# Expert stage of a two-block model: GpSimd asks for U and V rows one by one in turn, where a group asked for two of U and then two of V

## The chip, the cores and the metric

One Trainium2 chip, one of its cores. The time of a kernel is the device time of that core in microseconds (us), taken as the median of several runs. A profile is one further execution, recorded by the hardware profiler.

## The reference, cut to what matters

The model has two blocks of two layers each. The change touches the feed-forward of the first block, a mixture of 16384 experts per layer with 128 chosen for each token:

```python
def block(args):                       # 128 tokens
    hk, ek, gk = args                  # hk [128, 1024], ek, gk [128, 128]
    act = jax.nn.gelu(jnp.einsum('ted,td->te', u[ek], hk), approximate=False)
    return jnp.einsum('te,ted->td', gk * act, v[ek])
```

For each token and each of its 128 experts, one row of U (1024 floats, 4 KB) is multiplied with the token's row, and one row of V is added to the output with a weight. The experts come from eight heads with two top-16 searches and a top-16 of their sums each. Layer 0 does this for 512 tokens (256 of the context and 256 of x), layer 1 for 256 tokens: six tiles of 128 tokens.

## The kernel before, in words

The 128 tokens of a tile lie on the 128 partitions. A request is one indirect DMA that GpSimd issues. It brings the n-th expert's row for each of the 128 tokens: 128 rows of 4 KB, 524288 bytes, into one buffer. There are 6 buffers for U and 6 for V (`U_SLOTS`, `V_SLOTS`; only 4 for U while a projection still runs beside the first groups). Six tiles with 128 experts make 768 requests for U and 768 for V.

The work goes in groups of two experts (`GROUP = 2`), 384 groups in all. Each engine runs its own program in its written order and waits on semaphores:

- **GpSimd (POOL)** in group g waits until the dots of group g-3 have freed two U buffers (`dots_done`) and asks for two U rows (L1746). Then it waits until the weighing three groups before has freed two V buffers (`v_weighed`) and asks for the two V rows of group g-2 (L1756; `LAG = 2`).
- **VectorE (DVE)** waits for each U row in turn and multiplies and sums it with the token rows (L1782, called a dot here, one for each expert); after the second it signals `dots_done`. Then it multiplies the previous group's gelu by the gates (L1791), and does a piece of the searches for the experts of later groups (`keys.chunk`), in 13 of every 16 groups.
- **ScalarE (ACT)** in group g takes the gelu of the two dots (L1833), and then makes two diagonal matrices for group g-2 (L1842). So the diagonals of group g-2 come only after the dots of group g.
- **TensorE (PE)** weighs: it multiplies each diagonal by its V row into PSUM (L1890), four products of 128x512 a group, eight rows in the trace, and signals `v_weighed`.

SP loads the weights of the other stages, 2 MB apiece, through its own queue. In the first part of layer 0's expert stage it also loads the modulation weights (`w_mod`), which TensorE uses beside the experts.

The first groups of each layer run beside the projection and ask for U alone; the groups that follow catch up with three groups of V at a time. After that each turn of the loop asks for one group of U and one of V. The change is in these turns.

Of the kernel before, what the change touches and what calls it, by code (L numbers as in the profile page):

```python
# [330 lines left out]
class Angles:  # L331
# [51 lines left out]
    def gpsimd(self, pool):  # L383
        A = self.A
        pool.wait_ge(self.m.sines.sem, 1)
        for k in range(2):
            pool.tensor_scalar(A.sin[:, k, :], self.ang[:, 2 * k, :], A.const[:, C_SIGN + k:C_SIGN + k + 1], None, ALU.mult)
            pool.tensor_copy(A.cos[:, k, :], self.ang[:, 2 * k + 1, :])
# [1270 lines left out]
GROUP = 2  # L1659
U_FIRST = 4  # L1660
U_SLOTS = 6
V_SLOTS = 6
# [5 lines left out]
class Experts:  # L1668
# [63 lines left out]
    def turned(half):  # L1732
        return half // 4, slice((half % 4) * P, (half % 4 + 1) * P)

    def ask_u(self, pool, g):
        m = self.m
        if g % self.some == 0:
            pool.wait_ge(m.keys_done.sem, self.keys.base[m.keys_done] + g // self.some + 1)
            pool.sem_inc(m.rows_asked.sem, 1)
        needed = max(self.u_dots_needed(g * GROUP + r) for r in range(GROUP))  # L1740
        if needed:
            pool.wait_ge(m.dots_done.sem, self.at(m.dots_done, needed))
            pool.sem_inc(m.rows_asked.sem, 1)
        for r in range(GROUP):
            n = g * GROUP + r
            pool.indirect_dma_start(self.UROWS[self.u_slot(n)][:, :], None, m.dram["u"],  # L1746
                                    bass.IndirectOffsetOnAxis(ap=self.IDX[:, n:n + 1], axis=0)).then_inc(m.u_in[self.u_slot(n)].sem, 16)

    def ask_v(self, pool, v):
        m = self.m  # L1750
        if v * GROUP >= V_SLOTS:
            pool.wait_ge(m.v_weighed.sem, self.at(m.v_weighed, v - V_SLOTS // GROUP + 1))
            pool.sem_inc(m.rows_asked.sem, 1)
        for r in range(GROUP):
            n = v * GROUP + r
            pool.indirect_dma_start(self.VROWS[n % V_SLOTS][:, :], None, m.dram["v"],  # L1756
                                    bass.IndirectOffsetOnAxis(ap=self.IDX[:, n:n + 1], axis=0)).then_inc(m.v_in[n % V_SLOTS].sem, 16)

    def gpsimd(self, pool):
        m = self.m  # L1760
        for g in range(self.early):
            self.ask_u(pool, g)
        pool.wait_ge(m.psum_full.sem, self.last_product)
        pool.sem_inc(m.rows_asked.sem, 1)
        for v in range(self.v_until(self.early - 1)):
            self.ask_v(pool, v)
        for g in range(self.early, self.total + LAG):
            if g < self.total:
                self.ask_u(pool, g)
            for v in range(self.v_until(g - 1), self.v_until(g)):  # L1770
                self.ask_v(pool, v)

    def dots(self, dve, g):
# [295 lines left out]
class Mixer:  # L2069
# [9 lines left out]
    GROUP = {name: g for g, name in enumerate(ORDER)}  # L2079
# [1278 lines left out]
```

## Time and profile before

| | |
|---|---|
| time, median of 3 runs | 4158.63 us (4150.6 to 4171.39) |
| span of the profiled execution | 4275.6 us |
| GpSimd busy in the span | 1773.6 us (41%) |
| VectorE busy | 2421.0 us (57%) |
| TensorE matmul busy | 3480.2 us (81%) |
| GpSimd's requests | 768 for U, 768 for V, 805.40 MB |
| first and last U request | 491.4 and 3122.7 us |

The span runs from the first to the last instruction of the profiled execution, and is 117 us longer than the median of the runs. The expert stage of layer 0 ends at some 2050 us, and that of layer 1 begins at some 2380 us. Times inside the profile are counted from the start of the span. Busy time of GpSimd in these stages is the time in which it makes the descriptors of a request; the data moves later, on the core's 16 DMA engines.

### The profile page before, as it was taken

How to read it: one execution, taken by the hardware profiler on the slowest of the kernel's cores; microseconds unless marked ns; L12 is line 12 of the kernel's file. 1: busy time of each engine (PE TensorE's matmuls, PEld its weight loads, DVE VectorE, ACT ScalarE, POOL GpSimd, SP SyncE). 2: the span in 40 equal slices, each digit the busy share in tenths (PEclk: the TensorE clock that was granted, in tenths of full speed). 3: DMA queues.
4: the chain of work that ended last, by engine and by line, in shares of the span. 5: the costliest groups of instructions: out<-in, count | busy, mean ns of one | idle time of the engine just before them, and what ended most of it. 6: DMA issues, size and time to landing. Idle time of an engine off the chain costs nothing. (4 is left out here: it accounts for less than half of the span.)

```text
span 4275.6 us, 45081 instructions
## 1 busy us (share of the span) xinstructions
PE 3480.2 (81%) x15340; PEld 2243.2 (52%) x15340; DVE 2421.0 (57%) x5200; ACT 1342.5 (31%) x2777; POOL 1773.6 (41%) x1680
## 2 busy tenths in 40 slices
PE   7988878888887777767776777676779989999899
PEld 4855632223333222222576522222259879999699
DVE  3365545566556656654356655666555565655555
ACT  3264311111111111111355211111144554545543
POOL 0010466667777777777010477777720020000200
PEclk9999888999998999899888989999989999999999
DMA  5222389999999999999221799999954524544244
GB/s 196 97 80 108 137 305 384 397 405 404 388 397 373 369 351 365 356 359 369 83 99 58 274 363 371 362 360 359 365 197 167 189 79 158 188 165 178 79 165 151
DMA packets 246386, 1095.98 MB, mean 256 GB/s; under 512 B 27281, under 2 KB 30609, under 8 KB 227345
## 3 DMA queue, kind: packets, MB, share of 16 engines
q0 software_dynamic: 221184, 805.40, 49.7%
q1 hardware_dynamic: 24976, 287.73, 18.1%
q8 instruction: 123, 2.02, 0.2%
q14 instruction: 103, 0.84, 0.1%
HBM read 1091.97 MB, written 1.05 MB: 256 GB/s over the span
## 5 line engine op out<-in xcount | busy, mean ns | idle before, releaser
L1890 PE MATMUL ps<-v_rows,diagonal 128*128 128x512 f32 x3072 | 1558.1, 658 | 542.1 <-ACT diagonal L1842 262.0
L1782 DVE CUSTOM_DVE_ANT_0 u_rows<-u_rows,h_rows 128x1024 f32<-128x1024 f32 x768 | 939.8, 1227 | 870.9 <-DMA u_rows<-in_u,experts 791.0
L1890 PEld LDWEIGHTS ps<-v_rows,diagonal 128*128 128x128 f32 x3072 | 610.8, 208 | 1466.9 <-issue 1020.7
L1746 POOL DMA_INDIRECT u_rows<-in_u,experts x768 | 847.0, 1103 | 349.1 <-issue 218.0
L1756 POOL DMA_INDIRECT v_rows<-in_v,experts x768 | 791.4, 1031 | 381.9 <-issue 217.3
L1833 ACT ACTIVATE hidden<-hidden 128x2 f32<-128x2 f32 x384 | 78.0, 203 | 1827.0 <-DVEq L1784 1013.3
L2959 DVE TENSOR_TENSOR weights_low<-ring,weights_high 128x1024 fp32r<-128x1024 f32 (+2 forms) x344 | 396.9, 1162 | 378.6 <-ACT weights_high L2952 377.5
L2590 PE MATMUL ps<-h_high,weights_high 128*128 128x256 f32 x1664 | 486.5, 292 | 17.3 <-DVE h_low L2467 15.3
L2590 PE MATMUL ps<-h_low,weights_high 128*128 128x256 f32 x1664 | 474.4, 285 | 0.0
L2590 PE MATMUL ps<-h_high,weights_low 128*128 128x256 f32 x1664 | 474.1, 285 | 0.0
L2952 ACT ACTIVATE weights_high<-ring 128x1024 fp32r<-128x1024 f32 (+2 forms) x344 | 336.9, 988 | 140.9 <-PE ps L2590 71.6
L2590 PEld LDWEIGHTS ps<-h_high,weights_high 128*128 128x128 f32 x1664 | 322.5, 194 | 27.4 <-DVE h_low L2467 14.8
L2430 POOL TENSOR_TENSOR ret_q_k_g<-ret_q_k_g,cos 128x512 f32<-128x512 f32 x8 | 10.1, 1284 | 765.0 <-PE ps L2205 765.0
L2590 PEld LDWEIGHTS ps<-h_low,weights_high 128*128 128x128 f32 x1664 | 323.2, 194 | 1.2 <-issue 0.5
L2590 PEld LDWEIGHTS ps<-h_high,weights_low 128*128 128x128 f32 x1664 | 322.8, 194 | 0.0
L929 PE MATMUL ps<-h_high,weights_high 128*128 128x512 f32 (+1 forms) x704 | 257.1, 365 | 65.3 <-DVE weights_low L890 42.7
L890 DVE TENSOR_TENSOR weights_low<-ring,weights_high 128x1024 fp32r<-128x1024 f32 x112 | 136.2, 1225 | 245.4 <-ACT weights_high L873 243.2
L1842 ACT ACTIVATE diagonal<-const,hidden 128x128 f32<-128x128 f32 x768 | 258.6, 386 | 0.3
L929 PE MATMUL ps<-h_low,weights_high 128*128 128x512 f32 (+1 forms) x704 | 252.1, 358 | 0.0
L929 PE MATMUL ps<-h_high,weights_low 128*128 128x512 f32 (+1 forms) x704 | 251.2, 357 | 0.0
L2590 PE MATMUL ps<-hidden_high,weights_high 128*128 128x256 f32 x704 | 199.7, 284 | 7.6 <-DVE hidden_low L2675 7.6
L2590 PE MATMUL ps<-hidden_low,weights_high 128*128 128x256 f32 x704 | 198.8, 282 | 0.0
(363 smaller groups left out, 4344.8 us busy)
## 6 DMA issues: line engine op xcount, KB each, us to landing
ring<-in_ffn_gu SPq DMA_DIRECT2D x44, 2048.0 KB
ring<-in_w_in SPq DMA_DIRECT2D x26, 2048.0 KB
ring<-in_w_mod SPq DMA_DIRECT2D x24, 2048.0 KB
ring<-in_ffn_down SPq DMA_DIRECT2D x32, 1408.0 KB
ring<-in_peer_wq SPq DMA_DIRECT2D x8, 2048.0 KB
u_rows<-in_u,experts POOLq DMA_INDIRECT x768
v_rows<-in_v,experts POOLq DMA_INDIRECT x768
ring<-in_w_out SPq DMA_DIRECT2D x4, 2048.0 KB
```

The source lines that it names most:

```text
L890: dve.tensor_tensor(self.half(self.WL, j, n), self.piece(tile, n), self.half(self.WH, j, n).bitcast(F32), ALU.subtract)\
L929: mm = pe.matmul(A.ps[:, bank, 0:w_cols], w[:, k, :], x[:, k, c0:c0 + w_cols], start=(t == 0), stop=(t == len(terms) - 1))
L1746: pool.indirect_dma_start(self.UROWS[self.u_slot(n)][:, :], None, m.dram["u"], bass.IndirectOffsetOnAxis(ap=self.IDX[:, n:n + 1], axis=0)) ...
L1756: pool.indirect_dma_start(self.VROWS[n % V_SLOTS][:, :], None, m.dram["v"], bass.IndirectOffsetOnAxis(ap=self.IDX[:, n:n + 1], axis=0)).th ...
L1782: dve.tensor_tensor_reduce(rows[:, :], rows[:, :], self.HR[:, t, :], 1.0, 0.0, ALU.mult, ALU.add, self.HID[:, t % 2, s + r:s + r + 1])
L1833: act.activation(hid, hid, ACT.Gelu).then_inc(m.gelu_done.sem, 1)
L1842: last = act.activation(self.DIAG[:, (g % DIAGONALS) * GROUP + r, :], self.A.const[:, C_IDENT:C_IDENT + P], ACT.Copy, scale=self.HID[:, t ...
L1890: mm = pe.matmul(self.A.ps[:, self.banks(t) + half, :], self.DIAG[:, (g % DIAGONALS) * GROUP + r, :], rows[:, half * 512:(half + 1) * 512] ...
L2430: pool.tensor_tensor(X, X, bcast(A.cos[:, 0, :], 1, 2), ALU.mult)
L2590: mm = pe.matmul(self.psum(q), w[:, i, :], x[:, k, :], start=(self.opens(q) and i == 0 and w is h and x is high), stop=(self.ends(q) and k ...
L2952: act.activation(job.half(self.S.WH, q), job.source(self.slot(job, q), q), ACT.Copy).then_inc(self.m.split_high.sem, 1)
L2959: dve.tensor_tensor(job.half(self.S.WL, q), job.source(self.slot(job, q), q), job.half(self.S.WH, q).bitcast(F32), ALU.subtract)\
```

## The change

`ask_u` and `ask_v` are each split into a wait and the request for one row. Where a turn of the loop asks for one group of U and exactly one of V, a new `ask_pairs` issues U, V, U, V: the wait for U buffers stands ahead of the first U request as before, and the wait for V buffers stands ahead of the first V request, which is now the second of the four. Counts, buffers and semaphores stay as they were, and so do the other engines' programs.

```diff
+    def ask_pairs(self, pool, g, v):
+
+        self.u_wait(pool, g)
+        self.u_row(pool, g * GROUP)
+        self.v_wait(pool, v)
+        self.v_row(pool, v * GROUP)
+        for r in range(1, GROUP):
+            self.u_row(pool, g * GROUP + r)
+            self.v_row(pool, v * GROUP + r)
...
         for g in range(self.early, self.total + LAG):
+            asked = range(self.v_until(g - 1), self.v_until(g))
+            if g < self.total and len(asked) == 1:
+                self.ask_pairs(pool, g, asked[0])
+                continue
             if g < self.total:
                 self.ask_u(pool, g)
-            for v in range(self.v_until(g - 1), self.v_until(g)):
+            for v in asked:
                 self.ask_v(pool, v)
```

GpSimd's program in the middle of layer 0's expert stage, two groups of the kernel before (`u_rows` and `v_rows` are the buffers, `in_u` and `in_v` the tables, `experts` the list of rows):

```order
L1746 DMA u_rows_54<-in_u,experts 128x1024 [waits dots_done]
L1746 DMA u_rows_55<-in_u,experts 128x1024
L1756 DMA v_rows_76<-in_v,experts 128x1024 [waits v_weighed]
L1756 DMA v_rows_77<-in_v,experts 128x1024
L1746 DMA u_rows_56<-in_u,experts 128x1024 [waits dots_done]
L1746 DMA u_rows_57<-in_u,experts 128x1024
L1756 DMA v_rows_78<-in_v,experts 128x1024 [waits v_weighed]
```

The same place of GpSimd's program with the change:

```order
L1747 DMA u_rows_54<-in_u,experts 128x1024 [waits dots_done]
L1763 DMA v_rows_76<-in_v,experts 128x1024 [waits v_weighed]
L1747 DMA u_rows_55<-in_u,experts 128x1024
L1763 DMA v_rows_77<-in_v,experts 128x1024
L1747 DMA u_rows_56<-in_u,experts 128x1024 [waits dots_done]
L1763 DMA v_rows_78<-in_v,experts 128x1024 [waits v_weighed]
L1747 DMA u_rows_57<-in_u,experts 128x1024
```

The first V request and its wait moved one place ahead, and the second U request moved one place back, behind that wait. The first U request and the second V request stand where they stood.

## Rows read from the trace of the kernel before

**Rows 1.** The page, the span in 40 slices: GpSimd, DMA share, GB/s

```profile
POOL 0010466667777777777010477777720020000200
...
DMA  5222389999999999999221799999954524544244
GB/s 196 97 80 108 137 305 384 397 405 404 388 397 373 369 351 365 356 359 369 83 99 58 274 363 371 362 360 359 365 197 167 189 79 158 188 165 178 79 165 151
```

**Rows 2.** The page, costliest groups of instructions: the four of the expert stage

```profile
L1890 PE MATMUL ps<-v_rows,diagonal 128*128 128x512 f32 x3072 | 1558.1, 658 | 542.1 <-ACT diagonal L1842 262.0
L1782 DVE CUSTOM_DVE_ANT_0 u_rows<-u_rows,h_rows 128x1024 f32<-128x1024 f32 x768 | 939.8, 1227 | 870.9 <-DMA u_rows<-in_u,experts 791.0
...
L1746 POOL DMA_INDIRECT u_rows<-in_u,experts x768 | 847.0, 1103 | 349.1 <-issue 218.0
L1756 POOL DMA_INDIRECT v_rows<-in_v,experts x768 | 791.4, 1031 | 381.9 <-issue 217.3
```

**Rows 3.** GpSimd in three stretches: us, busy (instructions), PEclk, DMA share, GB/s

```profile
650.00:1300.00 650.00, 454.46 (x436) 0.92 1.00 396
1300.00:2050.00 750.00, 540.80 (x506) 0.91 0.95 356
2400.00:3130.00 730.00, 541.82 (x502) 0.92 0.97 363
```

**Rows 4.** GpSimd's groups from 1300 to 2050 us

```profile
L1746 POOL DMA_INDIRECT u_rows<-in_u,experts x250 | 277.9, 1112 | 76.2 <-issue 71.7 <-PE ps L1890 4.3 <-remote 0.3
L1756 POOL DMA_INDIRECT v_rows<-in_v,experts x256 | 263.7, 1030 | 118.2 <-issue 73.8 <-remote 28.9 <-PE ps L1890 15.5
```

**Rows 5.** The two requests' lines: duration, ns, min/median/max

```profile
L1746 POOL DMA_INDIRECT u_rows<-in_u,experts x768: 933/945/2172, 491.4 to 3122.7; - x192
...
L1756 POOL DMA_INDIRECT v_rows<-in_v,experts x768: 932/943/1982, 565.4 to 3133.4; - x192
```

**Rows 6.** GpSimd's waits, 1300 to 2050 us: us in total, times, longest

```profile
POOL v_rows L1756 <- remote: 28.9, 9, 4.1
POOL v_rows L1756 <- PE ps L1890: 15.5, 14, 3.9
```

**Rows 7.** The same, 2390 to 3140 us

```profile
POOL v_rows L1756 <- remote: 24.7, 9, 3.8
POOL v_rows L1756 <- PE ps L1890: 14.7, 12, 4.2
```

**Rows 8.** The same, 650 to 1300 us

```profile
POOL v_rows L1756 <- PE ps L1890: 41.5, 24, 9.2
POOL v_rows L1756 <- remote: 27.5, 9, 4.1
```

**Rows 9.** Timeline, start and us: a weighing, and the request for its buffer

```profile
1385.80 5.40 PE L1890 MATMUL ps<-v_rows,diagonal 128*128 128x512 f32 x8 [1.91 <-DMA v_rows<-in_v,experts]
...
1396.83 1.01 POOL L1756 DMA_INDIRECT v_rows<-in_v,experts  x1 [0.31 <-issue]
```

**Rows 10.** Timeline: two dots close together, and the requests beside them

```profile
1409.76 1.23 DVE L1782 CUSTOM_DVE_ANT_0 u_rows<-u_rows,h_rows 128x1024 f32<-128x1024 f32 x1 [4.01 <-issue]
...
1410.91 1.22 DVE L1782 CUSTOM_DVE_ANT_0 u_rows<-u_rows,h_rows 128x1024 f32<-128x1024 f32 x1
...
1410.50 1.29 POOL L1756 DMA_INDIRECT v_rows<-in_v,experts  x1 [3.90 <-remote]
1412.10 0.94 POOL L1756 DMA_INDIRECT v_rows<-in_v,experts  x1 [0.30 <-issue]
```

**Rows 11.** Timeline: two dots apart, and the requests beside them

```profile
1324.69 1.22 DVE L1782 CUSTOM_DVE_ANT_0 u_rows<-u_rows,h_rows 128x1024 f32<-128x1024 f32 x1 [1.63 <-DMA u_rows<-in_u,experts]
...
1326.77 1.22 DVE L1782 CUSTOM_DVE_ANT_0 u_rows<-u_rows,h_rows 128x1024 f32<-128x1024 f32 x1 [0.85 <-DMA u_rows<-in_u,experts]
...
1324.85 1.88 POOL L1746 DMA_INDIRECT u_rows<-in_u,experts  x1 [0.30 <-issue]
1327.03 1.78 POOL L1746 DMA_INDIRECT u_rows<-in_u,experts  x1 [0.30 <-issue]
```

More of the change, by code:

```diff
@@ L1733, in turned, with u_wait @@
         return half // 4, slice((half % 4) * P, (half % 4 + 1) * P)
-    def ask_u(self, pool, g):
+    def u_wait(self, pool, g):
         m = self.m
@@ L1743, in ask_u, with u_row, v_wait @@
             pool.sem_inc(m.rows_asked.sem, 1)
+    def u_row(self, pool, n):
+        m = self.m
+        pool.indirect_dma_start(self.UROWS[self.u_slot(n)][:, :], None, m.dram["u"],
+                                bass.IndirectOffsetOnAxis(ap=self.IDX[:, n:n + 1], axis=0)).then_inc(m.u_in[self.u_slot(n)].sem, 16)
+    def ask_u(self, pool, g):
+        self.u_wait(pool, g)
         for r in range(GROUP):
[L1745 to L1749, printed above, removed]
+            self.u_row(pool, g * GROUP + r)
+    def v_wait(self, pool, v):
         m = self.m
@@ L1753, in ask_v, with v_row @@
             pool.sem_inc(m.rows_asked.sem, 1)
-        for r in range(GROUP):
-            n = v * GROUP + r
-            pool.indirect_dma_start(self.VROWS[n % V_SLOTS][:, :], None, m.dram["v"],
-                                    bass.IndirectOffsetOnAxis(ap=self.IDX[:, n:n + 1], axis=0)).then_inc(m.v_in[n % V_SLOTS].sem, 16)
+    def v_row(self, pool, n):
+        m = self.m
+        pool.indirect_dma_start(self.VROWS[n % V_SLOTS][:, :], None, m.dram["v"],
+                                bass.IndirectOffsetOnAxis(ap=self.IDX[:, n:n + 1], axis=0)).then_inc(m.v_in[n % V_SLOTS].sem, 16)
+    def ask_v(self, pool, v):
+        self.v_wait(pool, v)
+        for r in range(GROUP):
+            self.v_row(pool, v * GROUP + r)
+    def ask_pairs(self, pool, g, v):
+        self.u_wait(pool, g)
+        self.u_row(pool, g * GROUP)
+        self.v_wait(pool, v)
+        self.v_row(pool, v * GROUP)
+        for r in range(1, GROUP):
+            self.u_row(pool, g * GROUP + r)
+            self.v_row(pool, v * GROUP + r)
     def gpsimd(self, pool):
```

## The prediction

> **What bounds the kernel now.** I begin with the slices of the page [rows 1]. From the sixth slice to the nineteenth and again from the twenty-fourth to the twenty-ninth the DMA engines are busy nearly all the time, and GpSimd stands at 6 or 7 tenths. The transfer rate is 384 to 405 GB/s at first and then falls to some 350 to 373, although the DMA row hardly shows it. So there are two regimes, and the stretches put numbers on them [rows 3]: from 650 to 1300 us the DMA share is 1.00 at 396 GB/s, and in the two later stretches it is 0.95 and 0.97 at 356 and 363 GB/s. The costliest groups [rows 2] say who waits: VectorE sat idle 791.0 us for U rows, while TensorE's idle time goes mostly to the diagonals that follow the dots. Everything in the stage hangs on when U rows land.
>
> Why do they land late in the second regime? GpSimd's own account from 1300 to 2050 us [rows 4] leaves no free time: 277.9 + 263.7 us of making requests, and 76.2 + 118.2 us idle before them, add up to 736.0 of 750 us. Of the idle time 145.5 us is "issue", 0.30 us ahead of nearly each of 506 requests. That is GpSimd's own pace, and it waits for nobody in it. A request takes 0.93 us at least and 0.94 us in the median [rows 5], so GpSimd can ask once in 1.24 us at best. A request is 524288 bytes, so this pace would give 423 GB/s. In the late stretches it asks once in 750/506 = 1.48 us and once in 730/502 = 1.45 us. The late regime is thus bound by GpSimd, the early one by the DMA engines with GpSimd waiting now and then. A change of the order costs or gives time in the late regime almost one for one, and in the early one only if the queue of requests runs dry.
>
> Two things stretch 1.24 to some 1.46 us. The first is waits at V requests, for a freed buffer or for something that the profile calls "remote" [rows 6, 7]. The second is that requests which meet a dot take longer. See the two dots close together [rows 10]: the first runs to 1410.99, and the request begun at 1410.50 takes 1.29 us, 0.36 over the minimum. The next request starts at 1412.10, when the second dot has 0.03 us left, and takes 0.94. See then two dots apart [rows 11]: the request at 1324.85, begun while the first dot runs to 1325.91, takes 1.88 us, and the one at 1327.03, begun under the second dot, 1.78. All three held requests end 0.80 to 0.82 us after their dot. GpSimd stands until the dot is over. I call this a collision.
>
> **The change part by part.** The number of requests, their size, and the number of waits stay (768 and 768). Nothing is added on VectorE, ScalarE, TensorE or SP. Four things move.
>
> (a) The wait for V buffers comes one request earlier, 1.24 us sooner in GpSimd's time, and what it waits for comes 1.24 us later: the second U row of a group is asked for one place later, the second dot ends that much later, and with it the gelu, the diagonals of two groups before, and their weighing. The room between "buffer free" and "request made" shrinks by 2 x 1.24 = 2.48 us. How much room is there? In one ordinary group [rows 9] the weighing that frees the buffer ends at 1385.80 + 5.40 = 1391.20, and the request comes at 1396.83. That is 5.6 us of room, less about 0.8 us between a freed buffer and a request that had waited for it (my estimate: the 0.3 us of issue and half a request of 0.94 us). Some 2.3 us of it would be left. So the ordinary group doesn't wait, and those that waited already wait longer. Behind the wait now stand three requests of the group, the second U row among them, for which VectorE waits; before, only the two of V stood there. In the two late stretches 18 waits are put down to "remote", 53.6 us in sum [rows 6, 7]. I charge each with the whole 2.48 us, since the cover that GpSimd has in requests handed over but not yet made is smaller by as much: 18 x 2.48 = 45 us. The 26 waits put down to TensorE there sum to 30.2 us, and 0.3 us of each is the usual issue time, so most are none. I charge them nothing. The bounds are 0 (the room suffices everywhere) and 44 x 2.48 = 109 us.
>
> (b) The same in the early stretch: 33 waits [rows 8]. There the DMA share is 1.00 [rows 3], so requests are queued ahead of the data, and a wait of a few us drains only the queue. I take 0. If that cover is gone, it is 33 x 2.48 = 82 us.
>
> (c) The two dots of a group stand apart. Before, the two U rows were asked for one behind the other and land 1.24 us or so apart, one dot's length (1.227 us, rows 2), so the two dots are one block. After a collision with the first, GpSimd's next request starts 0.82 + 0.30 = 1.12 us behind the first dot's end, just as the second dot ends, so that one is free [rows 10]. With U, V, U, V the rows land 2.48 us apart plus whatever a collision adds to the two requests between. Any collision with a V request is now inside the gap between two U requests. It pushes the second U row back by as much as it pushed GpSimd, so the second dot meets GpSimd's program at the same phase as the first did, and the collision is repeated. Before, this held only for collisions with a U request, and the pair 2.08 us apart [rows 11] is such a case, with both requests hit. The price: in the late stretches the requests take 540.80 + 541.82 us for 1008 [rows 3], against 1008 x 0.9325 = 940.0 at the minimum of rows 5. So collisions cost 142.7 us there. From rows 4, U has 277.9 - 250 x 0.933 = 44.7 us over its minimum and V 263.7 - 256 x 0.932 = 25.1, so V's share is 36%. Doubling that share adds 0.36 x 142.7 = 51 us. The bounds: the dots could fall into the gaps and all collisions vanish, -143 us. Or every late group (252 of them) becomes as bad as rows 11, with 0.95 + 0.85 = 1.8 us over the minimum against 142.7/252 = 0.57 now, +310 us. I take 51, near the first row's side, since the argument only repeats what V requests already pay.
>
> The Trainium skill has a rule on this point that speaks for less. "SBUF — State Buffer", section "Who interferes with whom", says that a VectorE instruction with two SBUF inputs contends only with a GpSimd instruction that reads SBUF, and the page's section "SBUF: two separate sides" tells of descriptor making that is locked out by another class of VectorE instruction. If a request were only a writer, the dot would not hold it up, term (c) would be 0 and the sum 45 us. Rows 11 show a request held to the end of the dot, so here the trace decides for the collision.
>
> (d) The first V row of a group lands one place earlier and the second where it did. TensorE waits for V rows now and then (1.91 us ahead of the weighing in rows 9). With the diagonals 1.24 us later, both V rows are there. That gives nothing, because the weighing starts with the diagonals, which are later.
>
> The sum: 45 + 0 + 51 = 96 us on the profiled execution of 4275.6 us, so 4372 us, or +2.2%. The runs shown have a median of 4158.6 us, 117 us under the profiled one. Some of the "remote" waits may belong to recording, so I take a little off and carry 91 us over: 4250 us.
>
> **The rivals.** *The DMA engines are the bound in all of it.* For it: a DMA share of 0.95 to 0.97 even in the late stretches [rows 3], and that the unprofiled runs are faster. Against it: 356 and 363 GB/s there against 396 in the early stretch, and GpSimd's account without free time. Then the order of requests that are queued anyway changes nothing: 4159 us, within 0.5%. The same result would come if (a) were covered and (c) found no new collisions. The Trainium skill speaks for this rival: "DMA: Bandwidth & Descriptors", section "Issuing engines are not separate DMA queues", has all DMAs run on the same 16 engines and interleave; by it alone, order would not matter.
>
> *The dots fall into the gaps.* Spaced 2.48 us, exactly two of GpSimd's paces, both dots can start just as a request starts. A dot of 1.23 us is then over before the next request needs the port 1.24 us later. As such a grid holds itself as long as DMA and GpSimd keep the same pace, collisions could vanish: -143 + 45 = -98 us, 4060 us. A third of it, 4125 us, is likelier. It decides when more than 45 of the 143 us go. Against it: a landing pace of 1.45 us instead of 1.24 shifts the phase at each row, and the pieces of the searches between the dots disturb it.
>
> *The bad phase holds.* Two collisions a group as in rows 11 keep themselves up, as the U rows then land apart by as much as the requests are held up. With half of the late groups in it, +155 + 45 = 200 us, 4359 us.
>
> **How the numbers follow.** The forecast has 0.60, the bad phase 0.08, no change 0.20 and the vanishing collisions 0.12. This gives slower by over 0.5% (21 us; about what a measurement of this kernel can tell from no change) 0.68, within it 0.20, and faster 0.12. The forecast's own range is 4185 to 4310 (45 us less or 60 us more). The range for 8 in 10 reaches from 4140, which takes in no change and a little of the faster case, to 4340, short of the bad phase.
>
> **What would show it.** Right: in the late stretches GpSimd's requests take more in the mean, with V's mean (1030 ns now) rising towards U's; dots of a group stand some 2.5 us apart; the waits at V requests are longer and more; GB/s falls below 356; the early stretch stays at 396. Wrong: GpSimd's mean falls towards 940 ns (vanishing collisions), or all of this holds, and the time is the same (the DMA engines bound it). What would upset the working most is if the room at V requests were eaten up in every group, since then each group pays, or if the waits called "remote" are absent without a profiler.

## The result, and the profile after

The changed kernel takes 4316.2 us (4305.44 to 4323.62, 4 runs) and the kernel before 4154.61 us: a ratio of 1.0369, with a 95% interval of 1.0333 to 1.0404. It is slower by 162 us. (Ratios in this text are estimates over the single runs, and can differ a little from the quotient of two medians.)

The page of the changed kernel, the slices and the costliest groups that answer to [rows 1, 2]:

```profile
span 4313.3 us, 45081 instructions
...
POOL 0010466767777777777101377777720020000200
...
DMA  5222499999999999999231699999954424445144
GB/s 194 98 95 91 142 327 372 390 373 379 373 383 366 361 363 357 350 343 381 115 118 49 239 349 363 361 365 375 370 208 159 180 82 173 177 162 188 70 168 154
...
L1763 POOL DMA_INDIRECT v_rows<-in_v,experts x768 | 881.1, 1147 | 348.8 <-issue 212.4
L1747 POOL DMA_INDIRECT u_rows<-in_u,experts x768 | 827.0, 1077 | 348.2 <-issue 215.8
```

GpSimd in the same three stretches as in [rows 3] (us, busy, clock, DMA share, GB/s):

```profile
650.00:1300.00 650.00, 458.08 (x416) 0.92 0.98 378
1300.00:2050.00 750.00, 579.17 (x512) 0.90 0.97 361
2400.00:3130.00 730.00, 539.78 (x487) 0.91 0.94 353
```

GpSimd's groups from 1300 to 2050 us, as in [rows 4]:

```profile
L1763 POOL DMA_INDIRECT v_rows<-in_v,experts x256 | 296.6, 1159 | 93.4 <-issue 73.0 <-PE ps L1916 20.4
L1747 POOL DMA_INDIRECT u_rows<-in_u,experts x256 | 282.7, 1104 | 78.1 <-issue 75.3 <-PE ps L1916 2.7
```

V requests have become the long ones: 1147 ns in the mean, against 1031 in [rows 2]. The rate of the early stretch has fallen from 396 to 378 GB/s, and its DMA share from 1.00 to 0.98.

One thing doesn't fit. This span, 4313.3 us, is only 37.7 us over the 4275.6 us of the profile before, while the times differ by 162 us. The changed kernel's profiled execution ran at its usual time (4315.28 us); the first profile of the kernel before belongs to none of its runs at 4155. Repeats point to the reason. The kernel before has two levels, near 4157 us and near 4305 us. In each of the later series all its executions lie on one level, profiled ones too, and the same chip has shown both. The first profile is the exception: its span is 25 us under that of the nearest profile of the upper level (4300.9 us). But its requests are as long (1103 and 1031 ns against 1100 and 1036), and it has the waits called "remote" that only the upper level shows. I count it with the upper level; the timed runs beside it are from the lower one. Each experiment below is compared with the kernel before of its own series.

### The profile page after: what moved, and what is told of

Same layout as the page of the kernel before. It is cut to its first block and busy times, and to the rows that moved or that the text cites. A ratio compares the mean times of both kernels' runs of the same rounds, so it can differ in the third digit from the quotient of the medians.

```text
span 4313.3 us, 45081 instructions
## 1 busy us (share of the span) xinstructions
PE 3487.6 (81%) x15340; PEld 2253.2 (52%) x15340; DVE 2422.3 (56%) x5200; ACT 1342.2 (31%) x2777; POOL 1841.3 (43%) x1680
## 5 line engine op out<-in xcount | busy, mean ns | idle before, releaser
L1763 POOL DMA_INDIRECT v_rows<-in_v,experts x768 | 881.1, 1147 | 348.8 <-issue 212.4
L1747 POOL DMA_INDIRECT u_rows<-in_u,experts x768 | 827.0, 1077 | 348.2 <-issue 215.8
L2616 PE MATMUL ps<-hidden_high,weights_low 128*128 128x256 f32 x704 | 200.3, 284 | 0.0
```

The costliest lines, as they stand in the source:

```text
L2616: mm = pe.matmul(self.psum(q), w[:, i, :], x[:, k, :], start=(self.opens(q) and i == 0 and w is h and x is high), stop=(self.ends(q) and k ...
```

## The experiments

**The kernel before, twice more, and the change beside it.** No edit.

> The kernel before, once more, for its profile. The first profile of it spans 4275.6 us against timed runs of 4155, while the changed kernel's profile (4313.3) and its time (4316) agree. If recording disturbs the late part of the expert stage (the waits called remote, requests at 1.45 us apart), this profile shows them again and spans about 4270. If that one execution was an outlier, this one spans about 4155 and shows late requests about 1.28 us apart. Time 4155 in both cases.

> The changed kernel once more, beside the kernel before on one chip. In the last series the kernel before took 4304.5 us, not 4155, while its two profiles span 4275.6 and 4300.9. If the first comparison was fair (3.7% slower), this one gives a ratio near 1.037, some 4464 us where the kernel before takes 4304. If the two had been timed under different conditions, the profiles count: 4313.3 against 4275.6 to 4300.9, a ratio of 1.003 to 1.009.

> The kernel before has now been seen at two levels, 4159 us (TensorE clock 0.94) on one chip and 4304.5 us (clock 0.93) on another, and both of its profiles come from the slower level. This run and the next share a chip. Wherever the kernel before runs at 4159, its profile shows the late expert stretches at about 1.3 us a request instead of 1.45, with fewer collisions and no long waits at V requests; where it runs at 4304, the profile repeats the first.

> The changed kernel on the same chip. It was 4316 and 4323 beside a kernel before at 4155 to 4159. If the chip itself is slower where the kernel before takes 4304, the change takes 4460 there, the ratio staying 1.037. If only the kernel before has two regimes (its requests locked in step with the dots, or not) and the new order has lost the good one, the change takes 4315 to 4330 everywhere, and the ratio is 1.003 to 1.006 beside 4304.

> The kernel before on the same chip, for its profile. All three profiles of it so far have waits called remote (27 to 39 of them) and belong to the 4304 level; the profiles of the changed kernel at 4316 and 4323 have none. If that level belongs to the chip, a kernel before that takes 4159 has no remote waits in its profile and some 1.35 us a request in the late stretches. Where it takes 4304 the profile repeats the first.

Measured, in five series:

| series | kernel before | changed kernel | ratio |
|---|---|---|---|
| first comparison | 4154.61 | 4316.2 | 1.0369 (1.0333 to 1.0404) |
| second | 4304.53, repeat 4305.86 | - | - |
| third | 4159.01 | 4322.73 | 1.04 (1.0363 to 1.0437) |
| fourth | 4307.61, repeat 4304.65 | 4379.07 | 1.0177 (1.015 to 1.0203) |
| fifth (same chip as the fourth) | 4156.23, repeat 4155.62 | - | - |

So neither simple expectation of the two levels holds. The changed kernel is slower at both levels, by 164 us at the lower and by 71 us at the upper, and it has two levels of its own that lie closer together (4323 and 4379). The level doesn't go with the chip: the fourth and the fifth series have one chip and two levels. It shows in the profile as waits called "remote". First GpSimd's waits in the kernel before on the upper level (4305.7 us), then in the changed kernel there (4376.6 us):

```profile
POOL v_rows L1756 <- remote: 120.2, 39, 4.5
```

```profile
POOL v_rows L1763 <- remote: 45.2, 17, 3.5
```

On the lower level neither kernel has one. What delays GpSimd in them I didn't find, only that it isn't the recording: runs without a profile have the same level.

The page of the kernel before on the lower level (fourth_before), which is the fair partner of the timed comparison:

```profile
span 4150.1 us, 45081 instructions
...
GB/s 201 84 99 92 131 294 393 419 401 396 402 403 393 394 398 399 382 388 374 61 102 72 280 391 403 405 394 371 399 130 173 158 84 163 193 164 170 88 171 147
...
L1746 POOL DMA_INDIRECT u_rows<-in_u,experts x768 | 818.6, 1066 | 347.5 <-issue 214.6
L1756 POOL DMA_INDIRECT v_rows<-in_v,experts x768 | 767.3, 999 | 307.4 <-issue 187.2
```

And of the changed kernel on that level, in the third series (again_after):

```profile
span 4313.4 us, 45081 instructions
...
L1763 POOL DMA_INDIRECT v_rows<-in_v,experts x768 | 883.4, 1150 | 347.6 <-issue 213.8
L1747 POOL DMA_INDIRECT u_rows<-in_u,experts x768 | 826.0, 1075 | 346.6 <-issue 217.9
```

These four lines are a ledger. Requests take 818.6 + 767.3 = 1585.9 us before and 883.4 + 826.0 = 1709.4 after, 123.5 us more. The idle time before them is 654.9 and 694.2 us, 39.3 more. The sum is 162.8 us, and the spans differ by 163.3. That the sum fits is no proof that GpSimd is the bound: the busy and idle time of any engine fill its stage. What the ledger tells is of which kind the added time is: three quarters longer requests and a quarter waits. On the upper level the same ledger gives 79.1 us more in requests, 9.2 less in waits, 69.9 in all, for spans 70.9 us apart. There the waits that were already long have absorbed a part.

Do the transfers themselves take longer when the two tables alternate? The medians from issue to landing say no. First fourth_before, then again_after:

```profile
u_rows<-in_u,experts POOLq DMA_INDIRECT x768, 6.4
v_rows<-in_v,experts POOLq DMA_INDIRECT x768, 6.3
```

```profile
u_rows<-in_u,experts POOLq DMA_INDIRECT x768, 6.2
v_rows<-in_v,experts POOLq DMA_INDIRECT x768, 6.2
```

Where are the longer requests? GpSimd and VectorE in the kernel before, lower level, timeline of two groups (start, us):

```profile
1500.73 0.94 POOL L1746 DMA_INDIRECT u_rows<-in_u,experts  x1 [0.30 <-issue]
1501.97 0.93 POOL L1746 DMA_INDIRECT u_rows<-in_u,experts  x1 [0.31 <-issue]
...
1500.68 1.30 DVE L1782 CUSTOM_DVE_ANT_0 u_rows<-u_rows,h_rows 128x1024 f32<-128x1024 f32 x1 [1.07 <-DMA u_rows<-in_u,experts]
1501.96 1.26 DVE L1782 CUSTOM_DVE_ANT_0 u_rows<-u_rows,h_rows 128x1024 f32<-128x1024 f32 x1
```

And in the changed kernel (again_after):

```profile
1507.39 1.99 POOL L1763 DMA_INDIRECT v_rows<-in_v,experts  x1 [0.30 <-issue]
1509.68 0.94 POOL L1747 DMA_INDIRECT u_rows<-in_u,experts  x1 [0.30 <-issue]
1510.93 1.11 POOL L1763 DMA_INDIRECT v_rows<-in_v,experts  x1 [0.30 <-issue]
...
1507.34 1.22 DVE L1808 CUSTOM_DVE_ANT_0 u_rows<-u_rows,h_rows 128x1024 f32<-128x1024 f32 x1 [2.02 <-DMA u_rows<-in_u,experts]
1510.00 1.23 DVE L1808 CUSTOM_DVE_ANT_0 u_rows<-u_rows,h_rows 128x1024 f32<-128x1024 f32 x1 [1.42 <-DMA u_rows<-in_u,experts]
```

Before, the dots start 0.05 us ahead of a request and 0.01 us ahead, and neither request is held up. With the change the dots are 2.66 us apart, and each holds up a request: the V request under the first to 0.82 us after the dot's end (1508.56), the one under the second to 0.81 after it (1511.23). I counted such requests (over 1.035 us) between the first dots of successive groups, over the 130 groups of requests 500 to 1020: 0.60 a group before, 1.36 with the change.

The request at 1500.73 us is free and the one at 1507.39 us is held, though both start 0.05 us after their dot. They lie on the two sides of a sharp edge. In all 14 traces no request that starts less than 0.045 us after a dot is held up, 276 of them, and each of the 4267 that start from there to 0.9 us after the dot's start is. Starts close to a dot's are common before and not with the change: of the 768 dots, 419 start between 0.045 us before and 0.255 us after the start of a request in fourth_before, and 253 in again_after. The kernel before on the upper level has already lost this phase: there it is 248 (third_before). That fits the smaller loss there. Whether the lost phase makes the upper level or follows from it is open.

**More room at the wait: 8 V buffers in place of 6, in both orders.** The space comes from fewer diagonals and one modulation row buffer.

```diff
-V_SLOTS = 6
+V_SLOTS = 8
...
-DIAGONALS = 4
+DIAGONALS = 2
...
-        rows = m.sb(ctx, "modulation_rows", [2, 2, 512])
+        rows = m.sb(ctx, "modulation_rows", [2, 1, 512])
```

> Old order, with 8 V buffers in place of 6 (the space comes from 2 pairs of diagonals in place of 4 and one modulation row buffer in place of 2). The V wait is now for the weighing four groups before and has 5 to 6 us more room. Room theory: no waits at V requests are left, faster than the kernel before by some of the 20 to 40 us of such waits, unless the smaller number of diagonals takes it back. Collision theory says nothing on it; it is the base for the next run.

> New order U, V, U, V with the same 8 V buffers. Room theory: with the room no longer short, the loss of the new order vanishes: same time as the old order with 8 V buffers. Collision theory: the loss by spaced dots stays, 40 to 50 us (about 1%) over the old order with 8 V buffers, with GpSimd's mean request longer by 0.05 us.

Measured: 4125.67 us in the old order, ratio 0.9932 (0.9906 to 0.9958) to the kernel before at 4159.01, and 4221.99 us in the new, 1.0159 (1.0114 to 1.0205). The page's groups of the two, old order first:

```profile
L1746 POOL DMA_INDIRECT u_rows<-in_u,experts x768 | 804.9, 1048 | 392.9 <-issue 231.5
L1756 POOL DMA_INDIRECT v_rows<-in_v,experts x768 | 765.1, 996 | 238.4 <-issue 229.4
```

```profile
L1763 POOL DMA_INDIRECT v_rows<-in_v,experts x768 | 880.0, 1146 | 240.5 <-issue 227.1
L1747 POOL DMA_INDIRECT u_rows<-in_u,experts x768 | 821.2, 1069 | 354.5 <-issue 225.0
```

Waits for freed V buffers are all but gone in both: of the 238.4 and 240.5 us of idle time before V requests, 229.4 and 227.1 are the issue time. The loss of the new order is still 96 us. V requests go from 996 to 1146 ns, as in the pair with 6 buffers (999 to 1150). So the room at the wait is not all of the loss. The requests alone take 131.2 us more in the new order; 36.3 us of it come back as shorter idle time, nearly all ahead of U requests (392.9 against 354.5 us). The expectation for the spaced dots, 40 to 50 us, was half of what they cost. The old order with 8 buffers beats both kernels of the case.

**The wait alone, moved.** The old order of requests, U, U, V, V, with the V wait ahead of the second U request (e_wait_early), or ahead of both (e_wait_first; its edit against the changed kernel):

```diff
     def ask_pairs(self, pool, g, v):
         self.u_wait(pool, g)
-        self.u_row(pool, g * GROUP)
         self.v_wait(pool, v)
-        self.v_row(pool, v * GROUP)
-        for r in range(1, GROUP):
-            self.u_row(pool, g * GROUP + r)
-            self.v_row(pool, v * GROUP + r)
+        self.u_row(pool, g * GROUP + 0)
+        self.u_row(pool, g * GROUP + 1)
+        self.v_row(pool, v * GROUP + 0)
+        self.v_row(pool, v * GROUP + 1)
```

> Requests in the old order U, U, V, V, but the wait for V buffers stands ahead of the second U request, as in the change. Room theory: the room at the wait shrinks by one place (1.24 us) instead of two, so about half of the loss: 4235 us. Collision theory (the dots stand apart): U rows still land together, so nothing but a rare wait: 4155 to 4175 us.

> Requests in the old order U, U, V, V, so the dots stay together, but the V wait stands at the head of the group, ahead of both U requests: the room at it shrinks by two places (2.48 us), exactly as in the change, and nothing else does. (In the run of V, V, U, U the room shrank by four places, not by two as expected there, since the U rows also came two later.) Room theory: all of the loss, 4323 where the kernel before takes 4159, or 4379 where it takes 4306. Both at work: the room's part alone, what is left of the change's loss when the 96 us of the pair with 8 V buffers are taken off, about 65 us where the kernel before takes 4159, and 30 to 50 us where it takes 4306. Collision theory alone: no loss.

Measured: 4318.12 us for the first, 1.0039 (1.0024 to 1.0053) to 4304.53, a loss of 14 us on the upper level, where half of the change's loss would be 36. The second has exactly the room of the change, and its dots together: those of a group start 1.27 us apart in the median between requests 500 and 1020, and 1.26 in fourth_before. It takes 4242.11 us, 1.0211 (1.017 to 1.0253) to 4156.23, a loss of 86 us, where 65 were expected if both causes are at work. GpSimd's groups on its page:

```profile
span 4267.3 us, 45081 instructions
...
L1747 POOL DMA_INDIRECT u_rows<-in_u,experts x768 | 878.8, 1144 | 456.6 <-issue 222.4
L1763 POOL DMA_INDIRECT v_rows<-in_v,experts x768 | 768.0, 1000 | 245.9 <-issue 194.8
```

Against fourth_before this is 47.6 us more idle time and 60.9 us more in requests, nearly all of that at the U requests, although nothing moved the dots apart. So the earlier wait comes with more than its own time. My reading is that dots and requests meet in another phase after it: 254 dots start near the start of a request, as counted above, against 419, and 0.78 requests a group are held up against 0.60. The run isn't a pure test of the room, since both U requests now stand behind the wait, and only one does in the change. (This profiled execution took 4269.17 us. Two of the six runs lie there and four near 4241; the median is 27 us under it.)

**Other orders.** V, U, U, V; U, V, V, U; and V, V, U, U, each with the V wait ahead of the first V request. The first of them, against the changed kernel:

```diff
     def ask_pairs(self, pool, g, v):
+        self.v_wait(pool, v)
+        self.v_row(pool, v * GROUP)
         self.u_wait(pool, g)
         self.u_row(pool, g * GROUP)
-        self.v_wait(pool, v)
-        self.v_row(pool, v * GROUP)
-        for r in range(1, GROUP):
-            self.u_row(pool, g * GROUP + r)
-            self.v_row(pool, v * GROUP + r)
+        self.u_row(pool, g * GROUP + 1)
+        self.v_row(pool, v * GROUP + 1)
```

> Order V, U, U, V: the two U rows stand together as before, but the V wait comes ahead of both, three places less room (3.7 us) where the change has two (2.5 us). Room theory: slower than the change, 4390 us. Collision theory: dots close together, each block of two collides once, so near the kernel before, 4155 to 4200 us.

> Order U, V, V, U: the second U row of a group and the first of the next stand together, the two of one group are three places apart. Room at the V wait: three places less, as in V, U, U, V. Room theory: 4390 us, the same as V, U, U, V. Collision theory: blocks of two dots again, so 4155 to 4200 us.

> Order V, V, U, U: the dots stand together as before; the V wait comes two places earlier against the U rows, so the room at it shrinks by 2.48 us, the same as in the change. Room theory: the same time as the changed kernel beside it. Collision theory: the same time as the kernel before (within 0.3%), and GpSimd's mean request as in the kernel before.

Measured: V, U, U, V 4397.15 us, 1.0241 (1.021 to 1.0272); U, V, V, U 4419.08 us, 1.0291 (1.026 to 1.0321), both to 4304.53; V, V, U, U 4525.16 us, 1.0899 (1.0848 to 1.095) to 4159.01. That is +93, +115 and +366 us. None is near the kernel before, so collisions alone can't be the theory. My count for V, V, U, U was wrong: from the second U request of a group to the V wait three turns later that depends on it, there are 13 places in the kernel before, 12 and 11 with the wait moved, 11 in the change, 10 in V, U, U, V and in U, V, V, U, and 9 in V, V, U, U. With 9 places GpSimd's waits for weighings at V requests sum to 418 us. Its V line on the page of V, V, U, U:

```profile
span 4518.1 us, 45081 instructions
...
L1763 POOL DMA_INDIRECT v_rows<-in_v,experts x768 | 795.1, 1035 | 616.5 <-PE ps L1914 418.1
```

U, V, V, U has its dots some three and a half us apart, and most requests held up (some 1.6 a group in the same count). GpSimd is busy 1882.2 us on its page and 1810.7 in V, U, U, V, 71.5 us more, yet the times differ by 22 us. Longer requests are again partly paid back by shorter waits: the idle time ahead of V requests is 393.6 us there and 456.1 in V, U, U, V.

## Why the prediction was right, and where it was off

The forecast was 4250 us; 4316.2 lies inside the range (4140 to 4340), and slower had the largest chance. But the loss was put at 91 us and is 162. The time lies outside the forecast's own range (4185 to 4310), and nearer to the bad phase (4359) than to the forecast. The direction and both mechanisms are shown; that the time fell inside the wide range owes something to luck, since one term was left out and the others were priced from a profile of the other level.

**What bounds the kernel.** Right for the late stretches, as far as the runs show: the loss is longer requests and waits of GpSimd, and its transfers take no longer. That the early stretch is different, bound by the DMA engines, was wrong as a ground for leaving it out. With the change it holds 416 requests, at 0.98 share and 378 GB/s. Fourth_before and e_v8_before hold there:

```profile
650.00:1300.00 650.00, 461.35 (x444) 0.92 1.01 404
```

```profile
650.00:1300.00 650.00, 466.41 (x461) 0.94 1.02 417
```

So a share of 1.00 at 396 GB/s, on which the prediction rested, was no ceiling: with more V buffers the same stretch moves 417 GB/s.

**(a) The room at the wait**, 45 us charged to 18 "remote" waits. The mechanism, less room by two places, is borne out: e_wait_first has that room with its dots together and loses 86 us. The place of the charge was wrong. The timed runs were on the level without "remote" waits, and in the late stretches of the changed kernel there are none. Waits as such grew by 39 us over the program. The 26 waits put down to TensorE and charged with nothing were misread: 30.2 us less 0.3 us each leaves 22 us, which is not none. The estimate of 0.8 us from a freed buffer to a request that had waited holds (0.81 at the least in every trace), and so does the room: from the end of the weighing to the V request there are 5.62 us in the median on the upper level, and 3.31 with the change (third_before, third_after). But the timed runs were on the lower level, where it was 4.03 before and 3.12 after (fourth_before, again_after), so there was less to give than the 5.6 us of one group showed. There 36 of 378 V requests came within 0.9 us of the weighing, and 60 with the change.

**(b) The early stretch**, 0 us, cover by queued requests. This is the term that failed. At 1.5625 us a request instead of 1.464, the 444 requests of that stretch cost 44 us more. The starts of the requests say the same: again_after is 41 us behind fourth_before at request 500, 99 us at the last of layer 0, and 161 at the last of all. Queued requests didn't cover it; in that stretch V requests take 1130 ns in the mean instead of 1030, and the waits for weighings sum to 72.0 us instead of 56.6. The bound named, 82 us, held.

**(c) Dots apart**, 51 us. The mechanism is shown by the pair with 8 buffers: next to no waits for V buffers, V requests longer by 150 ns, a loss of 96 us. The size was off for two reasons. It was worked out from the upper level, where V requests were already over their minimum by 0.1 us. On the lower level V requests stood at 999 ns, and 978 in the late stretch, so there was more to lose. And it was counted for the late stretches alone, while V requests of the early one are longer too. What replaces it is 123.5 us more in requests over the whole program. Part of it may be due to (a), as in e_wait_first. The two losses, 86 and 96 us, sum to 182, over the 164 measured with both. They were measured with different numbers of buffers, so how far they overlap isn't shown.

**(d) V rows earlier**: put at nothing; no run tests it alone. The second U request also stands one place later, so the wait for U buffers, which needs its dot, has one place less room. The prediction doesn't name this; it cost nothing, as the idle time ahead of U requests is 347.5 us before and 346.6 after.

**TensorE's clock.** The mean granted clock over the program is 0.941 in fourth_before and 0.929 in again_after, and TensorE's products for the experts take 638 ns and 660 in the mean, some 0.2 us more for the eight of a group. That comes on top of the 2.48 us of (a); no run separates it. With 8 V buffers hardly a wait for a weighing is left in either order, so it has next to no part in the 96 us.

**The level.** The 117 us between the first profile and the timed runs were put down in part to recording. The runs say otherwise: the profile shows the marks of another level. I could have seen in it a warning that the profile's late stretch isn't that of the timed runs. It happened to leave the sign alone.

**The rivals.** No change, since the DMA engines bound all of it: refuted by the time, and by landing times that didn't grow. Vanishing collisions: refuted, but the picture behind it was the kernel before. There, on the lower level, more than half of the dots fall near the starts of requests and few requests are held up, and the change broke that. The bad phase (4359 us): two or more held requests were counted in 42% of the groups between requests 500 and 1020, close to the half that it assumed. Only the price was lower: in those groups of again_after a held request is 0.53 us over the minimum, where it assumed 0.9. With its chance of 0.08 this rival was closer to what happened than the chance says. The rule of the Trainium skill in "SBUF — State Buffer", section "Who interferes with whom", would have made (c) nothing if a request were only a writer. The 4267 held requests and the e_v8 pair decide against that, unless the request's reading of its row list counts as the read that the rule asks for; no run tells the two apart.

## What to carry to other kernels

Where one engine both makes descriptors and stands still while VectorE runs a two-input instruction, the order of its requests bears on the phase between the two. Here it paid to keep the consumer's instructions back to back, so that a block of them holds up one request and not each of them one. Before moving a request or its wait, count the places between a release and the wait for it: one place cost 14 us here and three, in two other orders, 93 and 115 on the upper level; two cost 86 and four, in another order, 366 on the lower one. The two rows of figures don't compare, as the change itself lost 71 us on the one and 164 on the other. And if a profile's span differs by 3% from the timed runs, find out which runs it stands for before anything is summed on it.

## What the runs showed that I had not expected

- The same kernel has two levels, 4155 to 4159 and 4304 to 4308 us in the median, in different series, on one chip too. On the upper one GpSimd shows 27 to 39 waits called "remote", 81 to 120 us in sum (the first profile has the fewest); on the lower one none. The cause stays open.
- Whether the request or the dot gives way turns on 0.045 us. A request that starts up to that long after a dot isn't held up, and it is the dot that runs longer, 1.25 to 1.30 us instead of 1.23. One that starts later under the dot is held until 0.80 to 0.83 us after the dot's end. A dot that starts 0.03 us or more after a request takes its usual 1.22 to 1.23 us. Two-input instructions of the searches hold requests up in the same way (L1629 and L1634, 42 requests in each of fourth_before and again_after).
- Waits and held-up requests give time back to each other: 71.5 us more of GpSimd's busy time in U, V, V, U than in V, U, U, V became 22 us of the whole.
